# Two attention layers of a two-block transformer kernel: the order of their second halves, one norm instead of two, and two low parts on GpSimd

## The chip, the cores and the metric

The kernel runs on one core of a Trainium2 chip. The metric is the device time of one launch in microseconds. The engines are TensorE (PE, with its weight loads PEld), VectorE (DVE), ScalarE (ACT), GpSimd (POOL) and SyncE (SP), which issues the weight loads. Each works through its own queue in program order; between engines there are only the semaphore waits that the kernel writes.

## The reference

Float32, one sequence of 256 tokens, width 1024. A first block (SwiGLU, retention with neighbourhood attention, SwiGLU) is followed by a second one with two layers, MoBA and differential attention, each followed by an MLP with squared ReLU:

```python
for i in range(2):
    h = x * (1.0 + scale1) + shift1
    if i == 0:
        y = moba_attention(h, moba_w_in, moba_w_out)      # 16 heads of 64
    else:
        y = diff_attention(h, diff_w_in, diff_w_out, ...)  # 8 heads of two parts of 64
    x = layer_norm(ALPHA * x + (1.0 + gate1) * y, ln_g[i, 0], ln_b[i, 0])
    h = x * (1.0 + scale2) + shift2
    y = jnp.square(jax.nn.relu(h @ w_up)) @ w_down
    x = layer_norm(ALPHA * x + (1.0 + gate2) * y, ln_g[i, 1], ln_b[i, 1])
```

With 256 tokens MoBA is plain causal softmax attention. The differential layer forms softmax(q1 k1) - lambda softmax(q2 k2) per head, multiplies with v, and takes an RMS norm over the 128 columns of each head before the output projection.

## The kernel before

**Numbers in two parts.** Every float32 operand of a large matmul is split into a high part (rounded by ScalarE, `split_hi`) and a low part (the rest, by VectorE, `split_lo`), and a product is three matmuls: high by high, low by high, high by low (`three`, L498 to L500). Weights come in units of 128 x 2048 through a ring of six slots: a load (SyncE, 1 MB), `split_hi` (semaphore `w_hi`), `split_lo` in place over the raw values (`w_lo`), use by TensorE (`w_used`), which frees the slot. `split_lo` is one subtraction of two SBUF tensors.

**An attention layer** (`attention`, once for each engine) has twelve units for q, k, v in two column blocks, and four for the output projection, numbered `u0` to `u0 + 15`. After the entry, the loop over *slots* gives TensorE one unit per slot: two *tile halves* of twelve matmuls each, with attention work placed between the tile halves (the first list of a slot's entry in the table) and behind the second (the second list). The tables are `ATTENTION`, `MOBA_SLOTS` and `DIFF_SLOTS`. Their events are, for a pair of heads or a head c: H transposes of rotated heads, S scores (L887, L889), W transposes of the weights (L910: six in MoBA, three in the differential layer), O outputs (MoBA L922, L925; differential L930 to L932), T transposes of two normed chunks of outputs (L621, differential only). Slot 14 holds the last two units, the projection of the second half of the heads, as *last quarters* (`last_quarter`); ahead of and among them stand W7, O7, T2, T3 and some filler matmuls (`busy`, L959: four in MoBA, six in the differential layer), whose result nobody reads.

**The helpers of one pair c.** VectorE `scores` (adds the mask, row maxima, L2067), ScalarE `exps` (L1349), VectorE `shares` (MoBA: L2093, L2098) or `combine` (differential: L2078 to L2084), TensorE W, ScalarE `weights_out` (L1338), TensorE O, then in MoBA ScalarE `output_hi` (L1381) and VectorE `outputs` (L2152), in the differential layer ScalarE `squares` (L1359) and VectorE `outputs` (L2145). W and O each need the previous one's place in PSUM back. In the differential layer the norm follows: `norms` for two heads at a time in the first half, `last_sums`, `norm_root_of` (ScalarE, after a table load, L1428), `last_rstd` and `last_norm` in the second, and then T, `pair_his` (ScalarE, L1042) and `pair_los` (VectorE, L1481).

ScalarE and VectorE find their order in the same tables, by rules in their loops: events of a slot's second list are helped in the next slot, and `split_hi` and `split_lo` for the unit four slots ahead come once per slot. The last of them, unit `u0 + 18`, stands at the end, before the layer norm (VectorE `ln_part`: L1582 multiplies PSUM with a row in SBUF, L1588 adds x, two SBUF tensors, L1590 takes the moments). Behind the norm TensorE waits for the first transposed quarter of the next input, split in two by VectorE (L1493, L1494).

GpSimd issues the loads of the modulation weights and of rows, adds the mask to the bias of the first block (L2306, 128 x 512), and does two sums at the very end (L2351, L2353).

## Time and profile before

| | |
|---|---|
| median of 3 runs | 1231.01 us (1229.95 to 1232.24) |
| the profiled execution, its own time | 1230.47 us |
| its span | 1228.7 us |
| TensorE busy | 1200.2 us, 98% |
| VectorE busy | 948.5 us, 77% |
| ScalarE busy | 618.5 us, 50% |
| GpSimd busy | 100.4 us, 8% |
| mean granted clock of TensorE | 0.996 of 2.4 GHz |

The MoBA layer's second half lies at 690 to 728 us of the span, the differential layer's at 985 to 1030. In a timeline a row's first number is the start, the second the duration; matmul ends are modelled, and the next one begins before the printed end, so pieces of work on TensorE are measured from start to start. A bracket gives the idle time before an instruction and what ended it.

### The profile page before, as it was taken

How to read it: one execution, taken by the hardware profiler on the slowest of the kernel's cores; microseconds unless marked ns; L12 is line 12 of the kernel's file. 1: busy time of each engine (PE TensorE's matmuls, PEld its weight loads, DVE VectorE, ACT ScalarE, POOL GpSimd, SP SyncE). 2: the span in 40 equal slices, each digit the busy share in tenths (PEclk: the TensorE clock that was granted, in tenths of full speed). 3: DMA queues.
4: the chain of work that ended last, by engine and by line, in shares of the span. 5: the costliest groups of instructions: out<-in, count | busy, mean ns of one | idle time of the engine just before them, and what ended most of it. 6: DMA issues, size and time to landing. Idle time of an engine off the chain costs nothing. (4 is left out here: it accounts for less than half of the span.)

```text
span 1228.7 us, 14780 instructions
## 1 busy us (share of the span) xinstructions
PE 1200.2 (98%) x5795; PEld 984.6 (80%) x5795; DVE 948.5 (77%) x1371; ACT 618.5 (50%) x841; POOL 100.4 (8%) x138
## 2 busy tenths in 40 slices
PE   7999999999999999999999999999999997999997
PEld 6888887888778878888887768888888776888885
DVE  6789878876656689888786668898998787766656
ACT  7445336445764464343565556344346664634441
POOL 2010132001600010000000000000100000000000
PEclk9999999999999999999999999999999999999999
DMA  9999995644655489989466437788855642567540
GB/s 308 339 317 320 315 301 180 222 141 160 198 169 174 160 295 338 311 302 322 137 233 207 135 115 259 265 288 301 316 193 200 190 138 103 170 204 226 176 166 35
DMA packets 145206, 274.31 MB, mean 223 GB/s; under 512 B 6241, under 2 KB 76081, under 8 KB 145137
## 3 DMA queue, kind: packets, MB, share of 16 engines
q1 hardware_dynamic: 127280, 209.80, 50.7%
q0 software_dynamic: 17792, 63.56, 15.3%
q8 instruction: 46, 0.75, 0.3%
q14 instruction: 24, 0.19, 0.0%
q10 hardware_dynamic: 64, 0.02, 0.0%
HBM read 270.41 MB, written 2.93 MB: 222 GB/s over the span
## 5 line engine op out<-in xcount | busy, mean ns | idle before, releaser
L1472 DVE TENSOR_TENSOR lo_w<-w_raw,hi_w 128x2048 fp32r<-128x2048 f32 x197 | 448.0, 2287 | 70.5 <-ACT hi_w L1035 70.2
L1035 ACT ACTIVATE hi_w<-w_raw 128x2048 fp32r<-128x2048 f32 x197 | 374.2, 1916 | 42.9 <-DMA w_raw<-in_w_mix_out 11.6
L498 PE MATMUL ps<-hi_w,xT 128*128 128x512 f32 x912 | 365.8, 401 | 5.8 <-DVE xT L1494 3.4
L500 PE MATMUL ps<-lo_w,xT 128*128 128x512 f32 x912 | 357.1, 392 | 0.0
L499 PE MATMUL ps<-hi_w,xT 128*128 128x512 f32 x912 | 356.5, 391 | 0.0
L498 PEld LDWEIGHTS ps<-hi_w,xT 128*128 128x128 f32 x912 | 172.2, 189 | 46.1 <-issue 11.1
L500 PEld LDWEIGHTS ps<-lo_w,xT 128*128 128x128 f32 x912 | 171.8, 188 | 37.2
L499 PEld LDWEIGHTS ps<-hi_w,xT 128*128 128x128 f32 x912 | 172.4, 189 | 33.4
L498 PE MATMUL ps<-hi_w,hT_hi 128*128 128x512 f32 x480 | 188.5, 393 | 0.4 <-DVE hT_lo L1682 0.4
L500 PE MATMUL ps<-lo_w,hT_hi 128*128 128x512 f32 x480 | 187.0, 390 | 0.0
L499 PE MATMUL ps<-hi_w,hT_lo 128*128 128x512 f32 x480 | 186.9, 389 | 0.0
L702 PE MATMUL ps<-xT,hi_w 128*128 128x512 f32 x384 | 134.6, 396 | 0.0
L500 PEld LDWEIGHTS ps<-lo_w,hT_hi 128*128 128x128 f32 x480 | 90.1, 188 | 19.0
L498 PEld LDWEIGHTS ps<-hi_w,hT_hi 128*128 128x128 f32 x480 | 90.2, 188 | 18.6 <-DVE hT_lo L1682 0.9
L499 PEld LDWEIGHTS ps<-hi_w,hT_lo 128*128 128x128 f32 x480 | 90.2, 188 | 18.3
L701 PE MATMUL ps<-xT,lo_w 128*128 128x256 f32 x336 | 93.7, 279 | 0.0
L1698 DVE SCALAR_TENSOR_TENSOR piece_acc<-aux,c_act,piece_acc 128x512 f32<-128x512 f32 x119 | 89.3, 751 | 3.6
L1186 ACT ACTIVATE area<-ps 128x512 f32<-128x512 f32 x24 | 14.3, 598 | 135.3 <-PE ps L702 135.3
L702 PEld LDWEIGHTS ps<-xT,hi_w 128*128 128x128 f32 x384 | 70.2, 188 | 13.8
L1140 ACT ACTIVATE hT_hi<-ps 128x512 fp32r<-128x512 f32 x22 | 13.2, 598 | 111.1 <-PE ps L621 111.1
L701 PEld LDWEIGHTS ps<-xT,lo_w 128*128 128x128 f32 x336 | 63.4, 189 | 2.1
L1777 DVE TENSOR_TENSOR area<-ps,area 128x512 f32<-128x512 f32 x24 | 16.5, 689 | 48.8 <-ACT area L1186 48.8
(265 smaller groups left out, 1041.9 us busy)
## 6 DMA issues: line engine op xcount, KB each, us to landing
w_raw<-in_ffn_w_in SPq DMA_DIRECT2D x86, 512.0 KB
aux<-in_ada_w POOLq DMA_DIRECT2D x34, 1024.0 KB, 6.9
w_raw<-in_mlp_w_up SPq DMA_DIRECT2D x32, 1024.0 KB
w_raw<-in_mlp_w_down SPq DMA_DIRECT2D x32, 1024.0 KB
w_raw<-in_w_mix_in SPq DMA_DIRECT2D x26, 1024.0 KB
w_raw<-in_ffn_w_out SPq DMA_DIRECT2D x22, 1024.0 KB
area<-in_ada_w POOLq DMA_DIRECT2D x14, 1024.0 KB, 5.7
w_raw<-in_moba_w_in SPq DMA_DIRECT2D x12, 1024.0 KB
```

The source lines that it names most:

```text
L498: pe.matmul(dst, lhs_hi, rhs_hi, start=start, stop=False)
L499: pe.matmul(dst, lhs_lo, rhs_hi, start=False, stop=False)
L500: return pe.matmul(dst, lhs_hi, rhs_lo, start=False, stop=stop)
L701: pe.matmul(dst[:, 0:SEQ], wlo[:, k, cols], xT_hi[:, k, :], start=False, stop=False)
L702: mm = pe.matmul(dst, whi[:, k, cols], both, start=k == 0, stop=k == KD - 1)
L1035: act.activation(hi_w[:, ring_slot(u), :], w_raw[:, ring_slot(u), :], ACT.Copy).then_inc(w_hi, 1)
L1140: act.activation(hi[:, c0:c0 + 2, :], ps[:, off:off + 2 * SEQ].rearrange("p (c n) -> p c n", c=2), ACT.Copy).then_inc(hidT_hi, 1)
L1186: act.activation(turned_lo, pair[:, :, 1, :], ACT.Copy).then_inc(up_low, 1)
L1472: vec.tensor_tensor(lo_w[:, ring_slot(u), :], w_raw[:, ring_slot(u), :], hi_w[:, ring_slot(u), :].bitcast(F32), ALU.subtract).then_inc(w_l ...
L1698: ins = vec.scalar_tensor_tensor(out=acc, in0=row, scalar=c_act[:, c:c + 1], in1=acc, op0=ALU.mult, op1=ALU.add)
L1777: vec.tensor_tensor(turned_sum, pair[:, :, 0, :], turned_lo, ALU.add).then_inc(up_sum, 1)
```

## The change

The two layers' second halves (pairs 4 to 7) get an order written out by hand on ScalarE and VectorE; the tables remain for the first half and for TensorE. On TensorE: S5 to S7 stand one per half slot, up to the middle of slot 12; O6 and W7 come into the middle of slot 13, O7 (and T2) behind it; the filler matmuls are gone; in slot 14 the first two quarters follow each other, and T3 comes behind both. In the differential layer the RMS factors of the first four chunks are computed in one chain (`first_rstd`), and applied in two parts. ScalarE copies the last heads (k2T) instead of VectorE. The low parts of units `U_MLP2` and `U_MLP2 + 2` (`u0 + 16` and `u0 + 18` of the differential layer) are GpSimd's; TensorE waits for them on `side_lo`, for the others on `w_lo`, whose count leaves those two out (`low_ready`). The low part of `u0 + 17` there is two halves on VectorE.

```diff
-             (9, ["H2"], ["O2", "W3"]), (10, ["H3"], ["S4", "O3"]), (11, ["S5", "T0"], ["T1", "W4"]),
-             (12, ["S6"], ["O4", "W5"])]
-MOBA_SLOTS = ATTENTION[:11] + [(11, ["S5"], ["W4"]), (12, ["S6"], ["O4", "W5"]), (13, ["S7", "O5", "W6"], ["O6"]),
-                              (14, [], [])]
-DIFF_SLOTS = ATTENTION + [(13, ["S7"], ["O5", "W6", "O6"]), (14, [], [])]
+             (9, ["H2"], ["O2", "W3"])]
+MOBA_SLOTS = ATTENTION + [(10, ["H3", "O3"], ["S4"]), (11, ["S5"], ["W4", "S6"]), (12, ["O4", "W5", "S7"], ["O5", "W6"]),
+                          (13, ["O6", "W7"], ["O7"]), (14, [], [])]
+DIFF_SLOTS = ATTENTION + [(10, ["H3", "O3"], ["S4"]), (11, ["S5", "T0", "T1"], ["W4", "S6"]),
+                          (12, ["O4", "W5", "S7"], ["O5", "W6"]), (13, ["O6", "W7"], ["O7", "T2"]), (14, [], [])]
+SIDE_LOWS = (U_MLP2, U_MLP2 + 2)
...
+def lows(u):
+    return u + 1 - sum(v <= u for v in SIDE_LOWS)
...
+            def low_ready(u):
+                if u in SIDE_LOWS:
+                    pe.wait_ge(side_lo, SIDE_LOWS.index(u) + 1)
+                else:
+                    pe.wait_ge(w_lo, lows(u))
...
-                        weights_T(7)
-                        if not diff:
-                            busy(1, 4)
-                        outputs(7)
-                        if diff:
-                            busy(0, 6)
-                            outputs_T(2)
-                        pe.wait_ge(w_lo, u0 + 15)
+                        low_ready(u0 + 14)
                         last_quarter(0, 0, 0)
+                        low_ready(u0 + 15)
+                        last_quarter(1, 0, 0)
                         if diff:
                             outputs_T(3)
-                        pe.wait_ge(w_lo, u0 + 16)
-                        last_quarter(1, 0, 0)
                         last_quarter(0, 0, 2).then_inc(part_done, 1)
...
+                def last_heads_out():
+                    act.wait_ge(headT, hb + 4)
+                    act.wait_ge(headT_out, hb + 3)
+                    act.activation(k2T[1], bank(0, 2).rearrange("p (c n) -> p c n", c=4), ACT.Copy).then_inc(headT_out, 1)
...
+                project_out(4)
+                weights_out(3)
+                taken(2)
+                split_hi(u0 + 14)
+                last_heads_out()
+                taken(3)
+
+                exps(4)
                 if diff:
+                    pair_his(0)
+                    pair_his(1)
+                    exps(5)
+                    split_hi(u0 + 15)
+                else:
+                    split_hi(u0 + 15)
+                    exps(5)
+
+                weights_out(4)
+                project_out(5)
+                exps(6)
+                if diff:
+                    squares(4)
+                    weights_out(5)
+                    squares(5)
+                    exps(7)
+                    weights_out(6)
                     act.activation(table_in[:, 3:4], table_in[:, 0:1], ACT.Sqrt)
+                    norm_root_of(0)
                     squares(6)
                     weights_out(7)
-                    norm_root_of(0)
+                    split_hi(u0 + 16)
                     squares(7)
+                    pair_his(2)
                     norm_root_of(1)
-                    pair_his(2)
+                    split_hi(u0 + 17)
                     pair_his(3)
                     split_hi(u0 + 18)
                 else:
+                    weights_out(5)
+                    output_hi(4)
+                    exps(7)
+                    split_hi(u0 + 16)
+                    weights_out(6)
+                    output_hi(5)
+                    split_hi(u0 + 17)
+                    weights_out(7)
                     output_hi(6)
+                    output_hi(7)
                     split_hi(u0 + 18)
-                    weights_out(7)
-                    output_hi(7)
...
+            def split_lo_half(u, h):
+
+                cols = slice(h * UNIT // 2, (h + 1) * UNIT // 2)
+                vec.wait_ge(w_hi, u + 1)
+                ins = vec.tensor_tensor(lo_w[:, ring_slot(u), cols], w_raw[:, ring_slot(u), cols],
+                                        hi_w[:, ring_slot(u), cols].bitcast(F32), ALU.subtract)
...
+                def first_rstd():
+
+                    vec.wait_ge(at_out, 4)
+                    then(vec.tensor_tensor(head_sq[:, :, :], head_sq[:, :, :], head_eps[:, :, :], ALU.add))
+                    rsqrt(head_rstd[:, :], head_sq[:, :, :].rearrange("p c t -> p (c t)"), 4 * NT, 1.0 / P, 0.0)
+
+                def first_norm(n):
+
+                    vec.wait_ge(at_norm, n)
+                    heads = o2[:, :, 2 * n * P:(2 * n + 2) * P].rearrange("p t (c n) -> p t c n", c=2)
+                    factor = head_rstd[:, 2 * NT * n:2 * NT * (n + 1)].rearrange("p (c t) -> p t c", t=NT).unsqueeze(3)
+                    vec.tensor_tensor(heads, heads, factor.broadcast_to([P, NT, 2, P]), ALU.mult).then_inc(at_norm, 1)
...
+                outputs(2)
+                rotate(3)
+                split_lo(u0 + 14)
+                outputs(3)
                 if diff:
+                    first_rstd()
+                    first_norm(0)
+                    scores(4)
+                    first_norm(1)
+                    scores(5)
+                    combine(4)
+                    pair_los(0)
+                    pair_los(1)
+                    scores(6)
+                    combine(5)
+                    split_lo(u0 + 15)
+                    outputs(4)
+                    combine(6)
+                    scores(7)
                     outputs(5)
+                    last_sums(0)
                     combine(7)
-                    outputs(6)
-                    last_sums(0)
                     last_rstd(0)
                     last_norm(0)
+                    outputs(6)
                     outputs(7)
                     last_sums(1)
+                    pair_los(2)
                     last_rstd(1)
-                    pair_los(2)
                     last_norm(1)
+                    split_lo_half(u0 + 17, 0)
                     pair_los(3)
-                    split_lo(u0 + 18)
+                    split_lo_half(u0 + 17, 1)
                 else:
+                    scores(4)
+                    shares(4)
+                    scores(5)
+                    split_lo(u0 + 15)
+                    scores(6)
+                    shares(5)
+                    outputs(4)
+                    shares(6)
+                    scores(7)
+                    outputs(5)
+                    split_lo(u0 + 16)
                     shares(7)
                     outputs(6)
+                    split_lo(u0 + 17)
+                    outputs(7)
                     split_lo(u0 + 18)
-                    outputs(7)
...
+                if s == S_DIFF:
+                    for u in SIDE_LOWS:
+                        pool.wait_ge(w_hi, u + 1)
+                        pool.tensor_tensor(lo_w[:, ring_slot(u), :], w_raw[:, ring_slot(u), :],
+                                           hi_w[:, ring_slot(u), :].bitcast(F32), ALU.subtract).then_inc(side_lo, 1)
```

How it moves instructions, at three places. The lines of the changed kernel are other ones: L1472 is now L1486, L2152 is L2179, L2093 and L2098 are L2119 and L2124, L1582 is L1608.

VectorE, end of the MoBA layer, before: from the low part of unit 17 to the layer norm (L1472 low part of a unit, L2152 low part of an output, L2093 and L2098 shares, L1582 the norm).

```order
L1472 TENSOR_TENSOR lo_w<-w_raw,hi_w 128x2048
L2152 TENSOR_TENSOR xT<-ps,xT 128x256
L2093 RECIPROCAL inv<-total 128x4
L2098 TENSOR_TENSOR area<-area,inv 128x2x128
L2098 TENSOR_TENSOR area<-area,inv 128x2x256
L2152 TENSOR_TENSOR xT<-ps,xT 128x256
L1472 TENSOR_TENSOR lo_w<-w_raw,hi_w 128x2048
L2152 TENSOR_TENSOR xT<-ps,xT 128x256
L1582 TENSOR_TENSOR area<-ps,aux 128x512
```

VectorE, the same place, now:

```order
L2179 TENSOR_TENSOR xT<-ps,xT 128x256
L1486 TENSOR_TENSOR lo_w<-w_raw,hi_w 128x2048
L2119 RECIPROCAL inv<-total 128x4
L2124 TENSOR_TENSOR area<-area,inv 128x2x128
L2124 TENSOR_TENSOR area<-area,inv 128x2x256
L2179 TENSOR_TENSOR xT<-ps,xT 128x256
L1486 TENSOR_TENSOR lo_w<-w_raw,hi_w 128x2048
L2179 TENSOR_TENSOR xT<-ps,xT 128x256
L1486 TENSOR_TENSOR lo_w<-w_raw,hi_w 128x2048
L1608 TENSOR_TENSOR area<-ps,aux 128x512
```

The first L2179 is outputs(5). The low part of unit 16 now stands between it and shares(7), and that of unit 18 directly ahead of the norm.

TensorE, end of the differential layer, before: from the end of O5 to the first last quarter.

```order
L932 MATMUL ps<-area 128x128
L910 MATMUL ps<-ident,area 128x128 x3
L930 MATMUL ps<-area 128x128
L931 MATMUL ps<-area 128x128
L932 MATMUL ps<-area 128x128
L910 MATMUL ps<-ident,area 128x128 x3
L930 MATMUL ps<-area 128x128
L931 MATMUL ps<-area 128x128
L932 MATMUL ps<-area 128x128
L959 MATMUL ps<-xT 128x256 x6
L621 MATMUL ps<-ident,area 128x128 x4
L498 MATMUL ps<-hi_w,xT 128x512
```

TensorE, the same place, now (L942 to L944 are O7, L633 is T2, L510 to L512 last quarters):

```order
L512 MATMUL ps<-lo_w,xT 128x512
L942 MATMUL ps<-area 128x128
L943 MATMUL ps<-area 128x128
L944 MATMUL ps<-area 128x128
L633 MATMUL ps<-ident,area 128x128 x4
L510 MATMUL ps<-hi_w,xT 128x512
L511 MATMUL ps<-hi_w,xT 128x512
L512 MATMUL ps<-lo_w,xT 128x512
L510 MATMUL ps<-hi_w,xT 128x512
L511 MATMUL ps<-hi_w,xT 128x512
```

O6, W7 and the filler are gone from between O5 and O7; T2 follows O7 at once.

VectorE, end of the differential layer, before: the end of `last_rstd(1)`, `pair_los(2)`, `last_norm(1)`, `pair_los(3)`, the low part of unit 18, the norm.

```order
L2129 SCALAR_TENSOR_TENSOR newton<-newton,head_sq 128x4
L2130 SCALAR_TENSOR_TENSOR head_rstd<-newton 128x4
L1481 TENSOR_TENSOR xT<-ps,xT 128x256 x2
L2139 TENSOR_TENSOR area<-area,head_rstd 128x2x256
L1481 TENSOR_TENSOR xT<-ps,xT 128x256 x2
L1472 TENSOR_TENSOR lo_w<-w_raw,hi_w 128x2048
L1582 TENSOR_TENSOR area<-ps,aux 128x512
L1588 SCALAR_TENSOR_TENSOR area<-x,area 128x512
```

VectorE, the same place, now: from `last_norm(1)` on.

```order
L2166 TENSOR_TENSOR area<-area,head_rstd 128x2x256
L1493 TENSOR_TENSOR lo_w<-w_raw,hi_w 128x1024
L1507 TENSOR_TENSOR xT<-ps,xT 128x256 x2
L1493 TENSOR_TENSOR lo_w<-w_raw,hi_w 128x1024
L1608 TENSOR_TENSOR area<-ps,aux 128x512
L1614 SCALAR_TENSOR_TENSOR area<-x,area 128x512
```

`pair_los(2)` now comes ahead of `last_rstd(1)`. Two half low parts (unit 17) stand around `pair_los(3)`, and none of unit 18 is left here.

## Rows read from the trace of the kernel before

**Rows 1.** The page, busy time of TensorE: us, share of the span, instructions.

```profile
PE 1200.2 (98%) x5795; PEld 984.6 (80%) x5795; DVE 948.5 (77%) x1371; ACT 618.5 (50%) x841; POOL 100.4 (8%) x138
```

**Rows 2.** Timeline of TensorE, end of MoBA: start, us, instruction, [idle before <-releaser].

```profile
713.58 0.50 PE L887 MATMUL ps<-area 64*128 64x128 f32 x4
...
715.24 0.88 PE L910 MATMUL ps<-ident,area 128*128 128x128 f32 x6
...
718.79 0.65 PE L922 MATMUL ps<-area 128*64 128x256 f32 x4
...
720.74 0.85 PE L910 MATMUL ps<-ident,area 128*128 128x128 f32 x6 [1.08 <-DVE xT L2152]
...
721.34 0.72 PE L959 MATMUL ps<-xT 128*128 128x256 f32 x4
...
723.44 0.50 PE L498 MATMUL ps<-hi_w,xT 128*128 128x512 f32 x1
```

**Rows 3.** The same, VectorE, first instruction of MoBA's layer norm.

```profile
727.87 0.69 DVE L1582 TENSOR_TENSOR area<-ps,aux 128x512 f32<-128x512 f32 x1 [3.33 <-PE ps L500]
```

**Rows 4.** The same, TensorE, end of the differential layer and entry behind it.

```profile
1000.56 0.55 PE L910 MATMUL ps<-ident,area 128*128 128x128 f32 x3 [0.28 <-DVE area L2084]
...
1015.08 0.38 PE L930 MATMUL ps<-area 128*128 128x128 f32 x2
...
1015.75 0.49 PE L910 MATMUL ps<-ident,area 128*128 128x128 f32 x3
...
1021.43 0.63 PE L621 MATMUL ps<-ident,area 128*128 128x128 f32 x4 [0.27 <-issue]
...
1023.43 0.47 PE L498 MATMUL ps<-hi_w,xT 128*128 128x512 f32 x1 [1.38 <-DVE xT L1481]
...
1024.90 0.60 PE L621 MATMUL ps<-ident,area 128*128 128x128 f32 x4
...
1026.72 0.49 PE L498 MATMUL ps<-hi_w,xT 128*128 128x512 f32 x1
...
1039.17 0.77 PE L498 MATMUL ps<-hi_w,xT 128*128 128x512 f32 x1 [1.07 <-DVE xT L1494]
```

**Rows 5.** Stretches: us, busy (matmuls), granted clock, DMA share, GB/s.

```profile
1040.00:1042.00 2.00, 2.00 (x6) 0.50 0.00 0
```

**Rows 6.** Timeline of VectorE, then ScalarE, end of MoBA.

```profile
714.57 0.29 DVE L2067 CUSTOM_DVE_ANT_0 area<-ps,area 128x128 f32<-128x128 f32 x1 [2.11 <-PE ps L889]
...
715.68 2.29 DVE L1472 TENSOR_TENSOR lo_w<-w_raw,hi_w 128x2048 fp32r<-128x2048 f32 x1
...
719.23 1.03 DVE L2098 TENSOR_TENSOR area<-area,inv 128x256 f32<-128x256 f32 x2
...
717.13 0.40 ACT L1349 ACTIVATE area<-area,top 128x128 f32<-128x128 f32 x1
...
718.80 0.19 ACT L1349 ACTIVATION_READ_ACCUMULATOR area<-area,top 128x1 f32 x1
...
719.98 1.90 ACT L1035 ACTIVATE hi_w<-w_raw 128x2048 fp32r<-128x2048 f32 x1
...
721.78 0.80 ACT L1338 ACTIVATE area<-ps 128x768 f32<-128x768 f32 x1
```

**Rows 7.** Timeline of GpSimd and VectorE side by side, twice.

```profile
1216.95 1.29 POOL L2351 TENSOR_TENSOR area<-area,aux 128x512 f32<-128x512 f32 x1 [114.47 <-ACT area L1454]
...
1217.25 1.54 DVE L1588 SCALAR_TENSOR_TENSOR area<-x,area 128x512 f32<-128x512 f32 x1
...
337.70 2.29 DVE L1472 TENSOR_TENSOR lo_w<-w_raw,hi_w 128x2048 fp32r<-128x2048 f32 x1 [2.86 <-ACT hi_w L1035]
...
338.56 2.58 POOL L2306 TENSOR_TENSOR area<-area,na_mask 128x512 f32<-128x512 f32 x1 [1.77 <-DMA area<-rel_scratch]
```

**Rows 8.** The same, VectorE, second instruction of the differential layer's norm.

```profile
1030.96 0.69 DVE L1588 SCALAR_TENSOR_TENSOR area<-x,area 128x512 f32<-128x512 f32 x1
```

**Rows 9.** The same, ScalarE, table load in the differential layer.

```profile
1016.97 1.28 ACT L1428 ACT_TABLE_LOAD   x1
```

More of the change, by code:

```diff
@@ L904, in weights_T @@
                     pe.wait_ge(at_p, ab + c)
-                    if c % 4 == 0 or c == 7 and not diff:
+                    if c == 4 and not diff:
                         outputs_taken(c)
@@ L953, in modulation_rows_2 @@
                         .then_inc(mod_T, 1)
-                def busy(b, n):
-                    pe.wait_ge(at_m, ab + 8)
-                    for _ in range(n):
-                        pe.matmul(ps[:, b * BANK:b * BANK + SEQ], xT_hi[:, 0, 0:P], xT_hi[:, 0, :], start=True, stop=True)
                 def last_quarter(n, t, c):
@@ L2157, in pair_los @@
                     chunk_los(ch_o + 2 * n, 2, lambda k: base + k * SEQ, xT_hi, xT_lo, 2 * n)
-                before, last_between = [], []
-                for slot, between, events in DIFF_SLOTS if diff else MOBA_SLOTS:
-                    if slot == 14:
-                        continue
-                    for event in before:
-                        if event[0] == "T":
-                            pair_los(int(event[1:]))
-                    if diff and slot == 12:
-                        split_lo(u0 + 11 + AHEAD)
+                ready = combine if diff else shares
+                before = []
+                for slot, between, events in ATTENTION:
                     for event in before:
@@ L2172, in attention @@
                         x_update(S_MLP1, 1)
-                    for event in last_between:
-                        if event[0] == "S":
-                            (combine if diff else shares)(int(event[1:]))
                     for event in before:
```

92 lines of the change are left out of this document (25 added, 67 removed).

## The prediction

> **What bounds the kernel now.** I read the page first: TensorE is busy for 98% of the span [rows 1], so only three things can matter: matrix work removed, holes between its instructions, and its granted clock. Then I read TensorE in order of time at the end of both attention layers. Three pieces repeat there. In the MoBA layer a scores and an outputs piece together take 1.66 us (S7 and O5, 713.58 to 715.24), the six weight transposes 0.60 (720.74 to 721.34). From W6 to O6 there are 3.55, so a tile half of a slot, twelve matmuls, takes 2.95 [rows 2]. Then W7 waits 1.08, four filler matmuls are run, O7 waits again, and the last quarters begin at 723.44. The layer norm on VectorE begins at 727.87, with VectorE having waited 3.33 for TensorE [rows 3]. In the differential layer outputs take 0.67 and, by the same subtraction, weight transposes 0.33 and a tile half about 2.86. The second transposes of outputs (T2) stand at 1021.43, the first last-quarter matmul at 1023.43 after a 1.38 hole, T3 at 1024.90, the quarters behind it at 1026.72, and after the layer norm TensorE restarts at 1039.17, waiting for VectorE [rows 4]. There the clock is at 0.50 (1.2 GHz) and six matmuls fill 2 us [rows 5]; in both ends the path from TensorE through VectorE's norm back to TensorE is what counts.
>
> **MoBA, part by part.** Before O6 the new order holds the same pieces as the old one less one tile half, so TensorE reaches O6's place at 718.79 - 2.95 = 715.85 [rows 2]. Counting back from there over a half (2.95), W6 (0.60), O5 and S7 (1.66) and another half (2.95), W5 ends at 707.7.
>
> Now the helpers. Their durations are start to start [rows 6]: scores 1.11 and a last read, 1.2; exponentials from 717.13 to 718.99, 1.87; shares 1.03 and a small reciprocal, 1.2; a high part 719.98 to 721.78, 1.8; a low part 2.2 of its 2.29; a copy of weights 0.8, 0.7 when another instruction follows. ScalarE copies W5's weights (to 708.6) and takes O4's high part (256 columns, about 0.4, to 709.0). Only then may VectorE do outputs(4) (256 columns too, 0.4), which in the new order stands ahead of shares(6) (to 710.6) and scores(7) (to 711.8). Exponentials(7) end at 713.7, the high part of unit 16, now ahead of the copy of W6, at 715.5, the copy at 716.2, O5's high part at 716.6, outputs(5) at 717.0. O6 must wait for that: **a hole of 1.2**. Behind outputs(5) VectorE now has the low part of unit 16 (to 719.2) and only then shares(7) (to 720.4), for which W7 waits on TensorE: **a hole of 2.6**. W7, a half and O7 put the last quarters at 724.8, against 723.44: 1.4 later, although the two old waits and the filler are gone. The quarters to the norm took 4.43 (723.44 to 727.87); VectorE has the low part of unit 18 in front of the norm as well, whose high part ScalarE starts after O7 (725.3 to 727.1), so VectorE is free at 729.4. The norm starts **1.5 us later**. Nothing behind it is shortened, since the norm's order is unchanged.
>
> **Differential layer, TensorE.** When W6 stood at 1015.75 TensorE had all its tile halves behind it. At O7 it now has, besides these, W6, O6 and W7 (0.33 + 0.67 + 0.33) and, I take it, not the hole of 0.28 that it had at W4 (1000.56) and one of about that size at S5: O7 at 1016.5, T2 at 1017.2. Old T2 was at 1021.43, so the reordering is worth 4.2 us at this point. T2 to the matmul behind it is 2.0 (1021.43 to 1023.43), a bare chain through ScalarE and VectorE.
>
> **Differential layer, the two low parts on GpSimd.** GpSimd's 512-column sum at 1216.95 takes 1.29. VectorE's L1588, which reads two tensors of SBUF, begins 0.3 later and takes 1.54, and ends 0.55 after GpSimd has. The same instruction elsewhere takes 0.69 [rows 7, 8]. The other way round, at 338.56, GpSimd takes 2.58 and ends 1.15 after VectorE's low part has (337.70 + 2.29). So of the two, whichever comes second waits for the end of the other's instruction. A low part has 2048 columns: between 4 x 1.15 = 4.6 and 4 x 1.29 = 5.2; I take 4.6, since a start cost need not repeat. If instead it let VectorE in between pieces, it would cost VectorE nothing; that is the rival below. The Trainium skill ("GPSIMD Engine Reference", Specifications) says that GpSimd shares its SBUF interfaces with VectorE and contends with VectorE instructions that have two SBUF inputs; the rows just given agree. Its section 3.1 gives 4.5 us for this operation and size, which would make each hold 0.1 shorter.
>
> *Unit 16.* O5 stands at 1008.9 (1016.5 less W7, O6, W6, O5 and two halves). Its result is there 0.7 later; then ScalarE has squares 0.5, exponentials(7) 1.9, a copy 0.4, the square-root table 1.5 [rows 9], a root 0.2, squares 0.5, a copy 0.4 and the high part 1.8: 1016.9. (The small ones are my estimates from their column counts, beside the 0.4 and 0.8 of 128 and 768 columns [rows 6].) GpSimd holds SBUF from 1016.9 to 1021.5. VectorE comes to the sum of head_sq and head_eps, two SBUF tensors, at 1018.2, and the low parts of pair 2 are queued behind it. They start at 1021.6 instead of 1018.6, and the last quarters at 1022.2 rather than 1019.2. TensorE is idle from 1017.8 to 1022.2. Twelve matmuls (2.85) now precede T3, where six did: T3 at 1025.1, the rest at 1026.9 (1.82 after T3, as before), against 1026.72. **Of the 4.2 nothing is left.** *Clock.* The old 0.50 came behind the wait for the layer norm that ended at 1039.17, and cost six matmuls some 0.2 each, **1.2 us**. I expect the same again here, before T3: T3 at 1026.3. The Trainium skill ("TensorE: Matmul & The Clock Gate", Part 1) says idleness brings the half clock; the row has it.
>
> *Unit 18.* ScalarE's high part ends some 3.1 after T3 (0.63 result, 0.66 pair, 1.8): 1029.4. GpSimd holds SBUF to 1034.0. VectorE's norm begins earlier, does L1582 (a PSUM operand and one of SBUF, not held) and stands at L1588, to 1034.6. Before, L1588 ended at 1030.96 + 0.69 = 1031.65 [rows 8]. So the norm, and with it the restart, is **2.9 later** (1.7 without the clock).
>
> **What costs nothing.** One reciprocal root for four chunks instead of two: eleven small VectorE instructions fewer; I have no row of one on VectorE, ScalarE's read at 718.80 takes 0.19 [rows 6], so about 2 us, in a stretch where TensorE doesn't wait for VectorE. k2T's copy on ScalarE: about 1.1 (0.80 for 768 columns), inside the tile half that precedes S4. The two halves of unit 17's low part stand where VectorE waits for T3 and for the matmuls. Weight loads of unit 19 are released a few us later, and are used after the norm. No DMA is added.
>
> **Sum.** The profiled execution has 1230.47 us; 1.5 + 2.9 = 4.4 gives 1234.9. The runs' median lies 0.54 above it: **1235.4**. Differences under 0.2% (2.5 us) can't be told from none.
>
> **Rivals.**
> - *A, no extra low clock in the hole after T2* (15%): +3.2, 1234.3. Against it: this hole of 4.4 us has no work in it at all.
> - *B, MoBA's holes (1.2 and 2.6 with 0.8 of work between) cool it too* (20%): another 1.2, 1236.6.
> - *C, GpSimd and VectorE share SBUF in turns within an instruction* (17%): for: only one VectorE instruction in the trace was seen waiting, beside 512 columns, not 2048. Then the quarters are at 1019.2, T3 at 1022.0, the rest at 1023.9, the norm starts at 1025.5 since no low part of unit 18 is in its way, the restart comes 4.6 earlier, and with the hole before it closed the low clock at the restart goes: 5.8 gained, less MoBA's 1.5: 1226.7, faster. It decides as soon as both holds together cost under 1.5 instead of 3.0 and 3.4.
> - *D, the tiny sum is not held, the norm is* (12%): T3 at 1022.0, unit 18's hold ends 1029.7, L1588 1030.3, 1.4 earlier; 1231.1, no change.
> - *E, ScalarE is late enough in the differential layer for TensorE to wait at O6 and W7 as in MoBA* (6%): about 0.3 of slack each in my count; +1 to +2, 1237.
>
> **How the numbers follow.** The forecast itself has 30%, A 15, B 20, E 6: slower, 71%. D and half-sized cases: 12%. C: 17%. The range leaves out C and little else: from 1230.5 (D) to 1237.6 (B with holds of 5.2, 0.6 longer each); the likeliest case's own range is 1234 to 1237.
>
> **What would show it.** MoBA: TensorE holes before O6 and W7 in slot 13, norm start 1.5 later. Differential: a GpSimd instruction of 2048 columns of 4.6 or more; a VectorE 4-column sum of 3 us; L1588 of 3 to 4 us; a granted clock of 0.5 near the last quarters. Wrong: these two VectorE instructions at their old length, T3 near 1022, no clock below 1.00 at the restart.

## The result, and the profile after

The changed kernel took 1238.51 us (median of 4 runs, 1237.91 to 1239.35); the kernel before, run beside it, 1230.78 (4 runs, 1229.95 to 1232.24). The ratio is 1.0058, 95% interval 1.0047 to 1.0070: slower, 7.7 us (the interval is 5.8 to 8.6) against a forecast of 4.4 for the change, and above the range's 1237.6. The profiled execution has 1238.18 us, its span 1236.4, the mean granted clock is 0.992 (before 0.996).

The page of the changed kernel; [rows 1] is the line before.

```profile
PE 1203.4 (97%) x5785; PEld 987.1 (80%) x5785; DVE 946.2 (77%) x1357; ACT 619.9 (50%) x843; POOL 109.7 (9%) x140
```

TensorE has ten matmuls fewer (the fillers) and is busy 3.2 us longer: part of the loss is the clock. GpSimd has 9.3 us more, the two low parts.

**End of the MoBA layer**: timelines of TensorE, then of VectorE (start, us, instruction, idle time before it and what ended it), to be read beside [rows 2, 3, 6], and the windows (us, busy (matmuls), granted clock, DMA share, GB/s).

```profile
718.14 0.65 PE L934 MATMUL ps<-area 128*64 128x256 f32 x4 [0.87 <-ACT area L1337]
...
721.45 0.87 PE L922 MATMUL ps<-ident,area 128*128 128x128 f32 x6 [2.43 <-DVE area L2124]
...
726.59 0.65 PE L934 MATMUL ps<-area 128*64 128x256 f32 x4
...
727.39 0.50 PE L510 MATMUL ps<-hi_w,xT 128*128 128x512 f32 x1
```

```profile
717.62 0.42 DVE L2179 TENSOR_TENSOR xT<-ps,xT 128x256 fp32r<-128x256 f32 x1 [4.69 <-ACT xT L1380]
717.96 2.28 DVE L1486 TENSOR_TENSOR lo_w<-w_raw,hi_w 128x2048 fp32r<-128x2048 f32 x1
...
720.36 1.03 DVE L2124 TENSOR_TENSOR area<-area,inv 128x256 f32<-128x256 f32 x2
...
731.94 0.68 DVE L1608 TENSOR_TENSOR area<-ps,aux 128x512 f32<-128x512 f32 x1
```

```profile
722.00:724.00 2.00, 2.00 (x9) 0.64 0.00 0
724.00:726.00 2.00, 2.00 (x6) 0.51 0.00 0
```

The two holes are there, 0.87 before O6 and 2.43 before W7. The second ends when VectorE is through with shares(7) (L2124), and ahead of that stands unit 16's low part (717.96), behind 4.69 us in which VectorE did nothing. What the forecast did not have is the clock at 0.5 behind the holes: W7 to O7, one tile half, takes 5.14 instead of 3.55 (718.79 - 715.24, [rows 2]). The norm starts at 731.94 instead of 727.87.

**End of the differential layer**: TensorE, beside [rows 4], VectorE and GpSimd, beside [rows 8], and windows.

```profile
1021.15 0.60 PE L633 MATMUL ps<-ident,area 128*128 128x128 f32 x4
...
1025.74 0.47 PE L510 MATMUL ps<-hi_w,xT 128*128 128x512 f32 x1 [3.99 <-DVE xT L1507]
...
1030.15 0.60 PE L633 MATMUL ps<-ident,area 128*128 128x128 f32 x4
...
1031.96 0.50 PE L510 MATMUL ps<-hi_w,xT 128*128 128x512 f32 x1 [1.21 <-DVE xT L1507]
...
1043.57 1.97 PE L587 MATMUL ps<-ident,area 128*128 128x128 f32 x8 [3.16 <-ACT area L1072]
...
1046.46 0.76 PE L510 MATMUL ps<-hi_w,xT 128*128 128x512 f32 x1 [0.92 <-DVE xT L1520]
```

```profile
1014.61 0.15 DVE L2145 TENSOR_TENSOR head_sq<-head_sq,head_eps 128x4 f32<-128x4 f32 x1
...
1022.01 0.42 DVE L2172 TENSOR_TENSOR area<-ps,subln 128x256 f32<-128x256 f32 x1 [2.13 <-ACT aux L1358]
1022.35 2.91 DVE L2145 TENSOR_TENSOR head_sq<-head_sq,head_eps 128x4 f32<-128x4 f32 x1
1025.18 0.74 DVE L1507 TENSOR_TENSOR xT<-ps,xT 128x256 fp32r<-128x256 f32 x2
...
1034.42 4.06 DVE L1614 SCALAR_TENSOR_TENSOR area<-x,area 128x512 f32<-128x512 f32 x1
```

```profile
1020.75 4.50 POOL L2377 TENSOR_TENSOR lo_w<-w_raw,hi_w 128x2048 fp32r<-128x2048 f32 x1 [49.23 <-ACT hi_w L1034]
1033.33 4.61 POOL L2377 TENSOR_TENSOR lo_w<-w_raw,hi_w 128x2048 fp32r<-128x2048 f32 x1 [8.08 <-ACT hi_w L1034]
```

```profile
1026.00:1030.00 4.00, 4.00 (x12) 0.57 0.02 4
1044.00:1050.00 6.00, 5.08 (x16) 0.50 0.12 49
```

A sum of four columns (L2145) takes 2.91 us; the same line for the two chunks before, at 1014.61 with GpSimd idle, took 0.15. It ends at 1025.26, and GpSimd's instruction at 1025.25. L1614 takes 4.06 instead of 0.69 and ends 0.54 after GpSimd. L2172 and L1507, with one operand in PSUM, take what they always do, and L2172 does so in the middle of GpSimd's instruction. In the chain of waits that ended last these two stand with 2.84 and 4.07 us.

**Where 7.7 us are.** The same points in the two profiled executions, and what each stretch between two of them has lost:

| stretch | before | after | loss |
|---|---|---|---|
| to the entry of slot 10 of the MoBA layer (H3), up to which the code is the same | 689.79 | 690.54 | 0.8 |
| to the norm of the MoBA layer | 727.87 | 731.94 | 3.3 |
| to the entry of slot 10 of the differential layer (H3) | 986.95 | 991.00 | 0.0 |
| to the end of the norm's first L1588/L1614 | 1031.65 | 1038.48 | 2.8 |
| to the restart | 1039.17 | 1046.46 | 0.5 |
| to the next transposes on TensorE | 1047.45 | 1055.15 | 0.4 |

The first line is no part of the change. In the fourteen profiled executions of this text that entry lies between 689.64 and 691.37, earlier the sooner the clock rises at the program's start: from 12 to 18 us there are 22 matmuls in the kernel before, 19 in the changed one, and 17 to 27 in the others. How much of it is in the difference of the medians can't be told. The other lines make 7.0 us, which lies inside the interval as 7.7 does. The times below are set against this entry where it matters.

### The profile page after: what moved, and what is told of

Its sections match the earlier page's. It is cut to its first block, busy times and chain, and to the rows that moved or that the text cites. A ratio compares the mean times of both kernels' runs of the same rounds, so it can differ in the third digit from the quotient of the medians.

```text
span 1236.4 us, 14751 instructions
## 1 busy us (share of the span) xinstructions
PE 1203.4 (97%) x5785; PEld 987.1 (80%) x5785; DVE 946.2 (77%) x1357; ACT 619.9 (50%) x843; POOL 109.7 (9%) x140
## 4 chain that ended last, share of the span: by engine, by line
PE 90%; DVE 6%; ACT 2%; issue 1%; DMA 0%; ACTq 0%; DVEq 0%
PE ps L510 24%; PE ps L512 24%; PE ps L511 24%; PE ps L714 7%; PE ps L713 3%; PE ps L633 2%; DVE lo_w L1486 2%; ACT hi_w L1034 1%; PE ps L587 1%; PE ps L922 1%; PE ps L783 1%; PE ps L901 1%; PE ps L899 1%; ACT aux L1057 0%; PE ps L716 0%
## 5 line engine op out<-in xcount | busy, mean ns | idle before, releaser
L1486 DVE TENSOR_TENSOR lo_w<-w_raw,hi_w 128x2048 fp32r<-128x2048 f32 x194 | 440.9, 2286 | 67.6 <-ACT hi_w L1034 67.3
L510 PE MATMUL ps<-hi_w,xT 128*128 128x512 f32 x912 | 366.7, 402 | 9.5 <-DVE xT L1507 5.2
L512 PE MATMUL ps<-lo_w,xT 128*128 128x512 f32 x912 | 357.9, 392 | 0.0
L510 PEld LDWEIGHTS ps<-hi_w,xT 128*128 128x128 f32 x912 | 172.8, 189 | 50.8 <-issue 14.4
L512 PEld LDWEIGHTS ps<-lo_w,xT 128*128 128x128 f32 x912 | 172.4, 189 | 37.4
L510 PE MATMUL ps<-hi_w,hT_hi 128*128 128x512 f32 x480 | 189.1, 394 | 0.4 <-DVE hT_lo L1708 0.4
L512 PE MATMUL ps<-lo_w,hT_hi 128*128 128x512 f32 x480 | 187.6, 391 | 0.0
L510 PEld LDWEIGHTS ps<-hi_w,hT_hi 128*128 128x128 f32 x480 | 90.6, 189 | 19.1 <-DVE hT_lo L1708 0.9
L512 PEld LDWEIGHTS ps<-lo_w,hT_hi 128*128 128x128 f32 x480 | 90.4, 188 | 19.1
```

The lines of the kernel that those rows point to most:

```text
L510: pe.matmul(dst, lhs_hi, rhs_hi, start=start, stop=False)
L512: return pe.matmul(dst, lhs_hi, rhs_lo, start=False, stop=stop)
L1486: vec.tensor_tensor(lo_w[:, ring_slot(u), :], w_raw[:, ring_slot(u), :], hi_w[:, ring_slot(u), :].bitcast(F32), ALU.subtract).then_inc(w_l ...
```

## The experiments

Each is the changed kernel with the edit shown, timed beside the kernel before. Ratios are to the kernel before, with 95% intervals; the changed kernel itself stands at 1.0058.

| run | us, median (runs) | ratio |
|---|---|---|
| e1_moba_split16 | 1232.64 (11) | 1.0011 (1.0003 to 1.0020) |
| e2_sum_behind | 1235.38 (6) | 1.0032 (1.0020 to 1.0044) |
| e3_pieces | 1231.06 (11) | 0.9995 (0.9986 to 1.0004) |
| e4_all_vector | 1233.63 (11) | 1.0017 (1.0009 to 1.0026) |
| e5_fill_w7 | 1237.00 (5) | 1.0041 (1.0028 to 1.0053) |
| e6_side18 | 1234.95 (11) | 1.0027 (1.0018 to 1.0036) |
| e7_moba_pieces | 1226.45 (5) | 0.9960 (0.9948 to 0.9973) |
| e8_early_vector | 1223.36 (5) | 0.9932 (0.9919 to 0.9946) |
| e9_fill_t2 | 1237.11 (5) | 1.0046 (1.0034 to 1.0059) |
| e10_fill_both | 1236.33 (5) | 1.0038 (1.0025 to 1.0051) |
| e11_t3_first | 1222.61 (5) | 0.9932 (0.9919 to 0.9946) |
| e12_fill_long | 1234.21 (7) | 1.0028 (1.0016 to 1.0039) |

### MoBA: the place of unit 16 (e1_moba_split16)

```diff
                     output_hi(4)
+                    split_hi(u0 + 16)
                     exps(7)
-                    split_hi(u0 + 16)
                     weights_out(6)
...
                     scores(7)
+                    split_lo(u0 + 16)
                     outputs(5)
-                    split_lo(u0 + 16)
                     shares(7)
```

> Only the MoBA layer's order differs from the changed kernel: ScalarE makes the high part of unit 16 before exponentials(7), VectorE its low part before outputs(5), where both sat idle (2.75 us before 712.96 and 4.69 us before 717.62 in the changed kernel). Theory (holes from the order of the helpers, and the low clock comes from the holes): TensorE waits neither at O6 nor at W7, the granted clock stays 1.00 through the last slot, the last quarters begin near 722.2 instead of 727.39 and the norm near 726.7 instead of 731.94; 5.2 us less, 1233.3. Rival (the low clock in slot 13 has another cause than the holes): the holes go, the clock stays at half for some ten matmuls, 3.5 us less, 1235.0. Rival (the helpers are late anyway): at most 1 us less.

Measured 1232.64, 5.9 less than the changed kernel. In the window of MoBA's last slots TensorE never stops and the clock is whole, and the norm starts at 726.14 (5.8 earlier); windows of TensorE, then VectorE:

```profile
716.00:720.00 4.00, 4.00 (x26) 1.00 0.13 50
720.00:724.00 4.00, 4.00 (x22) 1.00 0.51 133
```

```profile
726.14 0.68 DVE L1608 TENSOR_TENSOR area<-ps,aux 128x512 f32<-128x512 f32 x1
```

Some 0.8 of the 5.8 are the start of the program, which was as short here as in the kernel before (slot 10 of the MoBA layer is entered at 689.75). So two instructions in the wrong place (unit 16's high part and its low part) cost 5.0 us, the low clock behind the holes included; with them moved, the new order of the MoBA layer is 1.7 faster than the old (726.14 against 727.87).

### MoBA: the clock alone (e5_fill_w7)

```diff
-                          (13, ["O6", "W7"], ["O7"]), (14, [], [])]
+                          (13, ["O6", "F8", "W7"], ["O7"]), (14, [], [])]
```

F8 is eight filler matmuls like those of the kernel before.

> As the changed kernel, with eight filler matmuls of 256 columns (they write a bank nobody reads) between O6 and W7 in the MoBA layer, in the hole in which TensorE waits 2.43 us for VectorE. The helpers are untouched, so the hole's end is too. Theory (the half clock of slot 13 comes from TensorE's idleness just before): the granted clock stays 1.00 between 720 and 728, the tile half behind W7 takes 2.8 us instead of 4.5 and the last quarters begin 1.7 earlier: 1236.8 against 1238.5. Rival (the clock falls for another reason): still half clock for some ten matmuls, and no change or slightly slower.

```profile
720.54 0.88 PE L922 MATMUL ps<-ident,area 128*128 128x128 f32 x6 [1.29 <-DVE area L2131]
```

```profile
720.00:724.00 4.00, 3.46 (x18) 1.00 0.00 0
724.00:728.00 4.00, 4.00 (x22) 1.00 0.70 202
```

As expected: clock 1.00, 1237.0. W7 comes as late as before (3.30 behind O6, 3.31 in the changed kernel), and 1.5 us are back. The two intervals overlap, so the medians alone would not show it; in the trace the norm starts 439.8 us behind the entry of MoBA's slot 10, not 441.4. So the half clock comes from TensorE's idle time and costs 1.6 here.

### What GpSimd's instruction holds (e2_sum_behind)

```diff
                     outputs(7)
+                    pair_los(2)
                     last_sums(1)
-                    pair_los(2)
```

> Only one swap in the differential layer: VectorE's low parts of pair 2 (a PSUM operand and one of SBUF) come ahead of the 4-column sum (two SBUF operands). Theory (GpSimd's 2048-column instruction holds VectorE's instructions with two SBUF operands, and only those, to its own end): the low parts run at once during GpSimd's instruction, the last quarters begin near 1023.2 instead of 1025.74, the sum is held instead behind them to 1025.3, T3 comes near 1027.4 instead of 1030.15 with the clock at 1.00, and L1614 is held again (3 to 4.6 us) and ends near 1035.8 instead of 1038.48: 2.7 to 3.5 us less, 1235.5. Rival (GpSimd's instruction holds every VectorE instruction): the low parts are as late as the sum was, no change (1238.5).

VectorE, then GpSimd:

```profile
1023.18 0.76 DVE L1507 TENSOR_TENSOR xT<-ps,xT 128x256 fp32r<-128x256 f32 x2
1023.86 2.10 DVE L2145 TENSOR_TENSOR head_sq<-head_sq,head_eps 128x4 f32<-128x4 f32 x1
...
1032.69 3.51 DVE L1614 SCALAR_TENSOR_TENSOR area<-x,area 128x512 f32<-128x512 f32 x1
```

```profile
1021.38 4.55 POOL L2377 TENSOR_TENSOR lo_w<-w_raw,hi_w 128x2048 fp32r<-128x2048 f32 x1 [49.31 <-ACT hi_w L1034]
```

The low parts with one SBUF operand run inside GpSimd's instruction at their usual length; the sum is held to 1025.96, and GpSimd ends at 1025.93. The time is 3.1 us less. One expectation failed: with holes of 1.38, 1.14 and 1.21 us the clock still fell to half, at 1030.8 instead of 1026.6. In the MoBA layer, which this edit does not touch, the low clock lasted longer in this execution than in the changed kernel's and cost 1.2 us more there, so its absolute times can't be set side by side with the other's.

### Four short instructions in place of one (e3_pieces)

```diff
-                        pool.tensor_tensor(lo_w[:, ring_slot(u), :], w_raw[:, ring_slot(u), :],
-                                           hi_w[:, ring_slot(u), :].bitcast(F32), ALU.subtract).then_inc(side_lo, 1)
+                        for k in range(4):
+                            cols = slice(k * UNIT // 4, (k + 1) * UNIT // 4)
+                            pool.tensor_tensor(lo_w[:, ring_slot(u), cols], w_raw[:, ring_slot(u), cols],
+                                               hi_w[:, ring_slot(u), cols].bitcast(F32), ALU.subtract).then_inc(side_lo, 1)
```

TensorE waits for the fourth.

> Only GpSimd's two low parts differ: each is done in four instructions of 512 columns instead of one of 2048. Theory (whoever comes second waits for the end of the other's instruction, so VectorE gets in between two of them): the 4-column sum is over within 1.3 us instead of 2.9, the last quarters begin near 1024, L1614 takes at most 2 us instead of 4.06; 3 to 5 us less, 1234.5. Rival (GpSimd starts its next instruction before a waiting VectorE instruction gets in): no change, 1238 to 1239. Rival (cost is the number of columns in all, in turns): no change either, and the waits are spread over more VectorE instructions.

VectorE, then GpSimd:

```profile
1023.21 0.92 DVE L2145 TENSOR_TENSOR head_sq<-head_sq,head_eps 128x4 f32<-128x4 f32 x1
1024.05 0.74 DVE L1507 TENSOR_TENSOR xT<-ps,xT 128x256 fp32r<-128x256 f32 x2
...
1025.41 1.22 DVE L2156 SCALAR_TENSOR_TENSOR newton<-newton,head_sq 128x4 f32<-128x4 f32 x1
...
1034.04 1.59 DVE L1614 SCALAR_TENSOR_TENSOR area<-x,area 128x512 f32<-128x512 f32 x1
```

```profile
1021.62 4.99 POOL L2379 TENSOR_TENSOR lo_w<-w_raw,hi_w 128x512 fp32r<-128x512 f32 x4 [49.38 <-ACT hi_w L1034]
1030.85 5.93 POOL L2379 TENSOR_TENSOR lo_w<-w_raw,hi_w 128x512 fp32r<-128x512 f32 x4 [4.24 <-ACT hi_w L1034]
```

The time is 7.4 us less, more than expected. Same work on the same engine: the sum takes 0.92, not 2.91, and L1614 0.73 at 1031.96 and 1.59 at 1034.04, not 4.06. So a waiting VectorE instruction does get in between two of GpSimd's. More of them wait now, each a little (L2156, four columns, 1.22), and GpSimd pays too: its two low parts take 5.0 and 5.9 us from first start to last end, not 4.50 and 4.61. From MoBA's norm to the restart there are 308.35 us against 314.52, and from there to the next transposes 6.92 against 8.69. These 1.8, and part of the 6.2, are the clock: it stayed at 1.00 through the whole end of this layer, where the changed kernel has two stretches at half.

### No low part on GpSimd, and one (e4_all_vector, e6_side18)

```diff
-SIDE_LOWS = (U_MLP2, U_MLP2 + 2)
+SIDE_LOWS = ()
...
                     last_norm(1)
-                    split_lo_half(u0 + 17, 0)
+                    split_lo(u0 + 16)
                     pair_los(3)
-                    split_lo_half(u0 + 17, 1)
+                    split_lo(u0 + 17)
+                    split_lo(u0 + 18)
```

> GpSimd does no low part: VectorE makes that of unit 16 behind the second late norm of the differential layer, that of unit 17 in one piece behind the low parts of pair 3, and that of unit 18 ahead of the layer norm. Theory (the two GpSimd instructions cost what they hold VectorE for, not what they take off it): the 4-column sum takes 0.15, the last quarters begin near 1023.2, T3 near 1026.1, the norm's L1614 ends near 1033.9 instead of 1038.48, and the time at the half clock after the restart is shorter: 5 us less, 1233.3. Rival (VectorE is what is short of time here, and its two more low parts of 2.2 us each come back on the path): within 1 us of the changed kernel, 1238.

Measured 4.9 less, as expected: the sum takes 0.15 and L1614 ends at 1034.48. One part of the expectation failed, the low clock after the restart: behind a hole of 2.64 us before the transposes eleven matmuls ran at half clock, not seven, and L1614's end to the next transposes takes 16.98, not 16.67.

e6_side18 has `SIDE_LOWS = (U_MLP2 + 2,)` and no last line.

> As e4_all_vector, but unit 18's low part goes back to GpSimd in one instruction of 2048 columns. Theory (whoever comes second waits): GpSimd's instruction must itself wait for the end of VectorE's low part of unit 17 and ends near 35.4 on this trace's clock of times; L1614 of the layer norm starts earlier than in e4_all_vector, since 2.2 us of work are gone from ahead of it, but is held to about 1036: 1 to 2 us slower than e4_all_vector (1233.6), about 1235; the early part, up to the last quarters, as in e4_all_vector. Rival (unit 16's hold alone was the loss, and unit 18 on GpSimd is a gain): 2 us faster than e4_all_vector, 1231.5.

```profile
1028.82 5.56 POOL L2377 TENSOR_TENSOR lo_w<-w_raw,hi_w 128x2048 fp32r<-128x2048 f32 x1 [57.60 <-ACT hi_w L1034]
```

```profile
1027.64 2.28 DVE L1486 TENSOR_TENSOR lo_w<-w_raw,hi_w 128x2048 fp32r<-128x2048 f32 x1
1029.84 0.68 DVE L1608 TENSOR_TENSOR area<-ps,aux 128x512 f32<-128x512 f32 x1
1030.55 4.38 DVE L1614 SCALAR_TENSOR_TENSOR area<-x,area 128x512 f32<-128x512 f32 x1
```

Measured 1234.95, as expected: 1.3 slower than with that low part on VectorE, ahead of the norm. The intervals of the two overlap, but the traces agree with the step: from the entry of MoBA's slot 10 to L1614's end there are 344.7 us, and 343.3 in e4_all_vector. The hold goes both ways here: GpSimd's 5.56 are 1.1 of waiting for L1486 (to 1029.92) and 4.5 of work, and L1614 waits for GpSimd in turn. So unit 18 on GpSimd gains nothing even alone, and the step from the changed kernel to e6_side18 prices unit 16's low part on GpSimd at 3.6, with the low clock that goes with its hold.

### The clock alone in the differential layer (e9_fill_t2, e10_fill_both, e12_fill_long)

```diff
+                        if diff:
+                            busy(1, 15)
                         low_ready(u0 + 14)
                         last_quarter(0, 0, 0)
...
+                        if diff:
+                            busy(1, 13)
                         for h in range(2):
                             x_quarter_T(s + 1, 0, h, zt)
```

e9_fill_t2 has the first piece, e10_fill_both both, e12_fill_long both with 32 and 25.

> As the changed kernel, with fifteen filler matmuls of 256 columns behind T2 in the differential layer, in the hole of 3.99 us in which TensorE waits for VectorE's held sum and the low parts behind it. Theory (this hole is what halves the clock in the first last quarters, seven matmuls at 0.43 us apart instead of 0.23): the clock stays 1.00 from 1026 to 1030, T3 comes 1.5 earlier and with it unit 18's high part, GpSimd's hold and the norm: 1237.0 against 1238.5, the low clock after the restart unchanged. Rival (the norm does not follow T3, since the hold of unit 18 is what ends last and starts from something else): no change, 1238.5.

> As e9_fill_t2, with thirteen more filler matmuls in the hole of 3.16 us before the transposes of the normed tile, at the end of the differential layer. Theory (the longer time at half clock behind the restart comes from the longer hole before it): the transposes and the matmuls behind the restart run at 1.00, 2 us less than e9_fill_t2: 1235.0. Rival (the 0.92 us hole behind the transposes is enough for the half clock): as e9_fill_t2, 1237.0, or slower by what the fillers delay.

e9_fill_t2 hit its number and not its mechanism, and e10_fill_both missed both. The fault is the experiments': one filler of 256 columns takes 0.12 us, not the 0.23 that the counts were made for, so holes of 2.27 us (both runs) and 1.57 us (e10_fill_both) stayed, and the clock fell in both places as before. The trace of e9_fill_t2 shows no gain at the restart (1046.35 against 1046.46) and its interval overlaps the changed kernel's, so its median's 1.4 says nothing. What the two runs do say is that the clock fell behind a hole of 2.27, in both of them.

> As e10_fill_both, with 32 and 25 fillers instead of 15 and 13: one takes 0.117 us there (16 of them in 1.76 us), so the earlier counts left 2.27 us of the hole behind T2 and 1.57 of that before the transposes open, and the half clock came all the same. These leave about 0.3 of each. Theory (the half clock comes from the open holes, and costs the path 1.5 us at the last quarters and 1.5 to 2 around the restart): granted clock 1.00 from 1020 to 1034 and from 1036 to 1054, T3 1.5 earlier, GpSimd's second instruction and the norm too, 3 us less than the changed kernel: 1235.4. Rival (the fillers keep the clock but the norm does not follow): clock 1.00, time of e10_fill_both, 1236.3. Rival (the clock falls there for another reason than idleness): half clock in the last quarters still, 1237.

```profile
1020.00:1034.00 14.00, 12.52 (x77) 1.00 0.23 76
1036.00:1054.00 18.00, 16.71 (x92) 1.00 0.32 117
```

The same windows of the changed kernel have 0.88 and 0.81. The next transposes on TensorE start at 1051.57, 3.6 earlier than in the changed kernel, and the ratio falls by 0.0030 (3.7 us). L1614 still takes 4.05: nothing but the clock is mended. The 3.6 are two parts: GpSimd's second instruction, and so the norm, comes 1.35 earlier (1031.98 against 1033.33), and 2.2 come back between L1614's end and the next transposes (14.4 us, 16.7 in the changed kernel). Of these 2.2 the kernel before had 1.4 too (15.8).

### Both mends, and a version that beats both kernels (e7_moba_pieces, e8_early_vector, e11_t3_first)

e7_moba_pieces is the two edits of e1_moba_split16 and e3_pieces together.

> Both mends together: unit 16's split one place earlier in the MoBA layer (e1_moba_split16) and GpSimd's low parts in four instructions each (e3_pieces). Theory (the two layers' losses are apart and add): 5.9 and 7.4 us less than the changed kernel, 1225.2, with the clock at 1.00 from the MoBA layer's end to the end of the differential layer's. Rival (what is gained in one place is waited for elsewhere, or a low clock comes back): 1228 or more.

Measured 1226.45, 5.1 less than the kernel before beside it: they nearly add. But of its five runs (1224.6 to 1228.7) the profiled one is the slowest, and there the clock fell twice, at 1020 and at 1037, behind a hole of 1.99 and behind two of 0.75 and 1.07. e3_pieces has the same holes, and there it did not fall, so the holes alone don't say which of the two happens.

e8_early_vector has the MoBA edit, `SIDE_LOWS = ()`, and in the differential layer, on ScalarE and on VectorE:

```diff
                     weights_out(5)
+                    split_hi(u0 + 16)
                     squares(5)
...
                     weights_out(7)
-                    split_hi(u0 + 16)
+                    split_hi(u0 + 17)
                     squares(7)
                     pair_his(2)
                     norm_root_of(1)
-                    split_hi(u0 + 17)
+                    split_hi(u0 + 18)
                     pair_his(3)
-                    split_hi(u0 + 18)
...
                     scores(7)
+                    split_lo(u0 + 16)
                     outputs(5)
...
                     outputs(6)
+                    split_lo_half(u0 + 17, 0)
                     outputs(7)
...
                     last_norm(1)
-                    split_lo_half(u0 + 17, 0)
+                    split_lo_half(u0 + 17, 1)
+                    split_lo_half(u0 + 18, 0)
                     pair_los(3)
-                    split_lo_half(u0 + 17, 1)
+                    split_lo_half(u0 + 18, 1)
```

> The MoBA order of e1_moba_split16, and in the differential layer no low part on GpSimd: ScalarE makes the high part of unit 16 in its 3.8 us of idle time before squares(5), that of unit 18 before it takes pair 3; VectorE the low parts in stretches in which it sat idle (unit 16 behind scores(7), units 17 and 18 in halves around outputs(7), the second late norm and pair 3). Theory (the reordering on TensorE is sound, and VectorE has room for all three if they stand where it waits): the norm begins as soon as TensorE is done, some 2.9 us before that of e4_all_vector, and the low clock after the restart is shorter: 1223 to 1224. Rival (one of the halves delays outputs(7) or pair 3): 1226.

```profile
1016.00:1032.00 16.00, 13.37 (x66) 1.00 0.36 110
1032.00:1048.00 16.00, 14.93 (x71) 1.00 0.27 101
```

```profile
1024.49 0.69 DVE L1608 TENSOR_TENSOR area<-ps,aux 128x512 f32<-128x512 f32 x1 [0.34 <-issue]
```

Measured 1223.36: 8.2 less than the kernel before (0.7%), 15 less than the changed one. The norm starts at 1024.49, the restart is at 1033.43 with the clock at 1.00. TensorE's order is the changed kernel's, so that order was sound (from slot 10 of the differential layer to T2 both take 30.1 us, the kernel before 34.5); what ScalarE, VectorE and GpSimd did around it lost the gain.

e11_t3_first puts `outputs_T(3)` back between the two first quarters, and `pair_los(3)` ahead of both halves of unit 18.

> As e8_early_vector, with T3 put back to where it was before the change, ahead of the second six last-quarter matmuls, and VectorE's low parts of pair 3 ahead of both halves of unit 18. Theory (six matmuls behind T3 cover its chain through ScalarE and VectorE, so the wait of 1.21 us behind T3 goes, and VectorE's halves then end last): the norm starts 0.5 us earlier and the time is 0.5 to 1 us less than e8_early_vector (1223.4): 1222.7. Rival (T3 must wait for the second late norm, 19.6 against a first place at 19.5 on that trace, or VectorE is late): no change.

Measured 1222.61, the same ratio as e8_early_vector: no change is shown, against 0.5 to 1 us expected. In the trace the wait of 1.21 behind T3 is gone, but the norm starts only 0.3 earlier from MoBA's norm (297.27 against 297.56), since VectorE is what ends last now. Runs from 1222.0 to 1225.0 can't tell 0.3.

## Why the prediction was wrong

- **MoBA, the holes: right.** Forecast 1.2 and 2.6, measured 0.87 and 2.43. Less the 0.8 from the program's start, W7 stands at 720.7 (forecast 720.4); the norm would have begun at 729.6 without the clock, against the forecast's 729.4. The first hole is shorter because two errors partly cancel: TensorE reached O6's place at 716.5, not 715.85, and the helpers were 0.3 late. e1_moba_split16 shows that the cause named, the place of unit 16's parts, is the cause.
- **MoBA, the clock: the step that failed.** The text had the half clock behind these holes as rival B, at 20% and 1.2 us, and left it out of the sum without a reason. It came in the profile of the changed kernel and in all seven experiments that keep MoBA's holes unfilled; it cost 1.6 (5.14 against 3.55). e5_fill_w7 takes it away and leaves the holes.
- **Differential layer, TensorE: right.** T2 is at 1021.15. Less the 4.05 us by which slot 10 of this layer is entered later, that is 1017.1; forecast 1017.2.
- **Unit 16: right.** With the same 4.05 taken off, the quarters start at 1021.7 (forecast 1022.2) and T3 at 1026.1 (forecast 1026.3 with its low clock); the sum is held for 2.8 us.
- **Unit 18: right.** L1614 ends at 1034.4 (forecast 1034.6): 2.8 late against 2.9.
- **Restart: the second term left out.** "The old 0.50 came behind the wait for the layer norm" was taken over unchanged. But the later norm also makes TensorE's hole before the transposes 3.16 instead of 1.59, so that they run at half clock themselves (1.97 instead of 1.36 busy), and seven matmuls behind the restart instead of five: 0.9 more. e12_fill_long takes it away, and the kernel before's own part with it.
- **Start of the program**: 0.8 in these two executions, which the change has no part in.
- **The range.** Its ends don't follow from the cases it names: rival D stands at 1231.1, not 1230.5, and B with two holds 0.6 longer is 1237.8, not 1237.6. The measured 1238.51 is outside either way.

The transposes before the restart in the kernel before, beside 1043.57 in the changed one:

```profile
1036.74 1.36 PE L575 MATMUL ps<-ident,area 128*128 128x128 f32 x8 [1.59 <-ACT area L1073]
```

Together 3.3 + 2.8 + 0.9 + 0.8 = 7.8, for 7.7; the forecast's own terms, 1.5 and 2.9, came as 1.7 and 2.8. Rival B came true, larger than its 1.2, and alone it would not have been enough. Of the rivals, C (turns within an instruction) fell by the 2.91 and 4.06, D by the 2.91, and A by the clock of 0.57. E did not occur: O6 and W7 in the differential layer had no hole of 0.2 us or more. "What costs nothing" held: none of these shows in a wait of TensorE.

The Trainium skill ("SBUF — State Buffer", Who interferes with whom) states the rule for the hold: a VectorE instruction with two SBUF inputs and a GpSimd instruction that reads SBUF contend for ports that one of them holds for its whole instruction, and a VectorE instruction with at most one SBUF input, outside the two-port modes, does not contend with GpSimd. The rows of e2_sum_behind and e6_side18 agree, the first with both halves of it, the second in both directions. The Trainium skill ("GPSIMD Engine Reference", 3.1) has 4.5 us for a float32 `tensor_tensor` add of 2048 columns on GpSimd; the subtraction here took 4.50.

## What to carry to other kernels

Before work goes to GpSimd, look at which VectorE instructions with two SBUF operands stand on the path in that time: each waits for the end of GpSimd's whole instruction, even a sum of four columns, and cutting the instruction in four gave back 7.4 us here, the clock's part with it. When a hand-written order is changed, place the weight splits in stretches where both helpers sit idle, not ahead of what TensorE waits for next. And price a long hole on TensorE, or several close together, twice, once for itself and once for the clock behind it: here the second price was 1.0 to 2.8 us. In every profiled execution with MoBA's holes of 0.87 and 2.43 left open it was paid.

## What was not expected of the hardware

Holes don't tell alone whether the clock falls. Followed by half clock were one of 3.99 us (the changed kernel), one of 2.27 (e9_fill_t2), one of 1.99 (e7_moba_pieces), and three of 1.38, 1.14 and 1.21 within 6 us (e2_sum_behind). Not followed by it were one of 2.00 (e3_pieces), two of 1.37 and 1.21 within 5 us (e8_early_vector), and five of 0.23 to 1.38, 3.5 us together within 8, with six filler matmuls among them (the kernel before, up to the quarters at 1023.43). What decides is open. It lasted from five matmuls (the kernel before, after the restart) to eleven (e4_all_vector, there) that start 0.43 us apart instead of 0.23, 1.0 to 2.2 us. The dearest was in the MoBA layer of e2_sum_behind, with transposes at half clock too: O6 to the norm took 15.05 us, and 12.22 in e5_fill_w7, where it did not fall.
